# Two model halves on one core: 512-column products and split evictions for the first half's FFN expansions, chunks 5 to 23

## The reference

```
def conv_ffn(x, w_up, conv_w, conv_b, w_down):
    h = causal_dwconv(x @ w_up, conv_w, conv_b)      # w_up 1024 x 6144, conv over 3 positions
    u, g = jnp.split(h, 2, axis=-1)
    return (u * jax.nn.gelu(g)) @ w_down             # w_down 3072 x 1024
...
h = h + conv_ffn(rms_norm(h, ffn_norm_g[l]), ...)    # l = 0, 1
```

## Time and profile before

| what | value |
|---|---|
| three runs | 1871.14, 1871.27, 1871.76 us, median 1871.27 |
| span of the profiled execution, first to last instruction | 1869.4 us |
| TensorE, VectorE, ScalarE, GpSimd busy | 98%, 77%, 52%, 11% of the span |
| instructions | 31793, of them 13284 matmuls |
| memory traffic | 334.67 MB, mean 179 GB/s |

### The profile page before, as it was taken

The page is one execution under the profiler, slowest core; times in us unless marked ns, Lnnn a source line. Parts: engine busy times, 40 slices in busy tenths (PEclk is TensorE's granted clock), DMA queues, the critical chain, the costliest instruction groups (busy, mean ns, idle before and its releaser), DMA issues.

```text
span 1869.4 us, 31793 instructions
## 1 busy us (share of the span) xinstructions
PE 1831.9 (98%) x13284; PEld 1725.2 (92%) x13284; DVE 1436.2 (77%) x1707; ACT 972.1 (52%) x1174; POOL 204.1 (11%) x160
## 2 busy tenths in 40 slices
PE   7999999999999999999999999999999999999997
PEld 7889998999999998899999998889888999999887
DVE  7987996598998578758965797759775896678764
ACT  6356665385665355544453555535553445445542
POOL 2001321000432030002200010001000320001000
PEclk9999999999999999999999999999999999999999
DMA  7324555435555545554454454544555445445551
GB/s 290 133 102 158 190 188 186 181 136 181 192 192 181 203 158 192 203 214 150 166 201 161 158 203 181 202 181 176 186 202 203 158 175 192 155 164 206 191 206 65
DMA packets 46789, 334.67 MB, mean 179 GB/s; under 512 B 5184, under 2 KB 5568, under 8 KB 6464
## 3 DMA queue, kind: packets, MB, share of 16 engines
q1 hardware_dynamic: 46512, 332.20, 49.2%
q0 software_dynamic: 144, 0.52, 0.1%
HBM read 331.65 MB, written 1.05 MB: 178 GB/s over the span
## 4 chain that ended last, share of the span: by engine, by line
PE 82%; DVE 10%; ACT 3%; POOL 2%; DMA 1%; issue 1%; SPq 0%; DVEq 0%; ACTq 0%
PE psum L277 24%; PE psum L280 12%; PE psum L261 11%; PE psum L263 11%; PE psum L262 11%; PE psum L301 6%; DVE w_lo L243 3%; PE psum L308 3%; POOL scratch L1746 1%; DMA w_raw<-stream_in 1%; POOL x_resid L391 1%; ACT w_hi L234 1%; DVE scratch L328 1%; POOL scratch L1743 1%; PE psum L597 1%
## 5 line engine op out<-in xcount | busy, mean ns | idle before, releaser
L234 ACT ACTIVATE w_hi<-w_raw 128x2048 fp32r<-128x2048 f32 x313 | 597.1, 1912 | 422.2 <-PE psum L263 158.1
L243 DVE TENSOR_TENSOR w_lo<-w_raw,w_hi 128x2048 fp32r<-128x2048 f32 x313 | 724.2, 2316 | 39.8 <-ACT w_hi L234 39.8
L261 PE MATMUL psum<-x_split,w_hi 128*128 128x256 f32 x1896 | 541.0, 285 | 13.8 <-DVE x_split L423 10.4
L263 PE MATMUL psum<-x_split,w_lo 128*128 128x256 f32 x1896 | 537.0, 283 | 0.0
L262 PE MATMUL psum<-x_split,w_hi 128*128 128x256 f32 x1896 | 537.0, 283 | 0.0
L277 PE MATMUL psum<-x_split,w_hi 128*128 128x512 f32 x1088 | 384.6, 399 | 0.0
L261 PEld LDWEIGHTS psum<-x_split,w_hi 128*128 128x128 f32 x1896 | 364.4, 192 | 15.2 <-issue 14.6
L262 PEld LDWEIGHTS psum<-x_split,w_hi 128*128 128x128 f32 x1896 | 364.4, 192 | 0.5
L263 PEld LDWEIGHTS psum<-x_split,w_lo 128*128 128x128 f32 x1896 | 364.3, 192 | 0.0
L280 PE MATMUL psum<-x_split,w_lo 128*128 128x256 f32 x1088 | 305.6, 281 | 0.0
L277 PE MATMUL psum<-h_split,w_hi 128*128 128x512 f32 x816 | 288.6, 399 | 0.0
(11 more groups left out here) (249 smaller groups left out, 2411.8 us busy)
## 6 DMA issues: line engine op xcount, KB each, us to landing
w_raw<-stream_in SPq DMA_DIRECT2D x313, 1024.0 KB, 4.8
x_resid<-x_in SPq DMA_DIRECT2D x1, 1024.0 KB, 6.9
y_out<-x_resid SPq DMA_DIRECT2D x4, 256.0 KB, 2.5
scratch<-mask_in SPq DMA_DIRECT2D x1, 768.0 KB, 10.9
scratch<-ev_in SPq DMA_DIRECT2D x1, 512.0 KB, 9.5
scratch<-inv_in POOLq DMA_DIRECT2D x1, 512.0 KB, 6.1
params<-par_in SPq DMA_DIRECT2D x1, 247.0 KB, 7.1
matrices<-mat_in SPq DMA_DIRECT2D x1, 192.0 KB, 8.9
```

The lines of the kernel that those rows point to most:

```text
L234: act.activation(w_hi[:, n % RING, :], raw[:, n % RAWS, :], ACT.Copy).then_inc(hi_ready, 1)
L243: dve.tensor_tensor(w_lo[:, n % RING, :], raw[:, n % RAWS, :], w_hi[:, n % RING, :].bitcast(F32), ALU.subtract).then_inc(lo_ready, 1)
L261: pe.matmul(dst, w_hi[:, c.slot, b:b + P], src[:, k0 + k, 0, :], start=opens, stop=False)
L263: done = pe.matmul(dst, w_lo[:, c.slot, b:b + P], src[:, k0 + k, 0, :], start=False, stop=last and k == nk - 1 and m == len(tiles_) - 1)
```

## The change

`up0` and `up1` join the list of wide phases. Their chunks 5 to 23 (19 in each) are then issued wide, take two events each, and go through the three-step eviction. The count by which the three steps are signalled covers the two new phases, and ScalarE's first tap waits for the scaled sum.

```diff
-WIDE = ("upA", "upB")
+WIDE = ("up0", "up1", "upA", "upB")
...
-FIRST = [("ev_in", 13, 13), ("ev_out", 4, 4), ("up0", FF1, FF1), ("down0", 12, 7),
+FIRST = [("ev_in", 13, 13), ("ev_out", 4, 4), ("up0", FF1, 2 * FF1 - NARROW), ("down0", 12, 7),
...
-         ("up1", FF1, FF1), ("down1", 12, 7)]
+         ("up1", FF1, 2 * FF1 - NARROW), ("down1", 12, 7)]
...
         def wide_count(c):
-            return (WIDE.index(c.phase) + 2 * c.layer) * (FF2 - NARROW) + c.n - NARROW + 1
+            first = {"up0": 0, "up1": FF1 - NARROW, "upA": 2 * (FF1 - NARROW),
+                     "upB": 2 * (FF1 - NARROW) + FF2 - NARROW}[c.phase]
+            return first + 2 * c.layer * (FF2 - NARROW) + c.n - NARROW + 1
...
             def taps(c):
                 w, b = conv
-                act.wait_ge(*taken(c.event))
+                act.wait_ge(*scaled(c))
```

## The result

The changed kernel takes 1881.43 us (median of four runs, 1880.24 to 1882.01) against 1871.20 us before (median of four as well); the ratio is 1.0049, with a 95% interval of 1.0037 to 1.0061. It is slower by 0.5%. The profiled execution took 1880.24 us.

The account below looks back on a forecast made before the run. TensorE was taken to bound the kernel, VectorE right behind it and setting the pace of up0 and up1 after the change. Late starts of 3.88 + 5.16 = 9.04 us on 1871.27 gave 1880.3 us, range 1874.5 to 1884.7.

Parts of the forecast that it names:

- The bound: In up0 and up1 TensorE sets the pace without gaps, VectorE close behind, needing 5.35 us against 5.76 a chunk.
- TensorE's gain of 0.11 us a chunk: In up0 and up1, 38 chunks go from 5.76 to 5.65 us, 4.2 us of gain if nothing else holds TensorE.
- VectorE's period: Per wide chunk of up0 and up1: 5.35 - 0.60 + 1.33 = 6.08 us, over TensorE's 5.65, so VectorE sets the pace.
- GpSimd's share: In up0 and up1, GpSimd's two instructions per chunk lengthen VectorE's four taps from 1.66 to 2.63 us, by 0.97.
- the fourth case: Much slower rival: GpSimd falls on the scaling, 0.38 us each round, period 6.46, loss 21.9 us, 1893 us; chance 0.05.
- Where the waits begin: TensorE waits for banks from chunk 11 of up0 and chunk 8 of up1, some 13 and 16 waits of 0.43 us.
- The hand-over: In up0 and up1, from the end of VectorE's addition to TensorE's start on the freed banks: 0.14 us.
- The starts of the contractions: down0 starts at 294.78, 3.88 us late; down1 at 590.92 against 585.76, 5.16 us late.
- The last hidden tile: Ready at 310.95 in down0, read by TensorE at 311.02; just holds, a miss costing some tenths of a us per phase.
- The sum: Whole kernel: 3.88 + 5.16 = 9.04 us slower, span 1878.4 us, time 1880.3 us.

Follow-up runs that it names:

- experiment 1: The changed kernel without VectorE's scaling in up0 and up1, chunks 5 to 23 left unscaled: 1865.99 us, ratio 0.9968 against the kernel before.
- experiment 2: The changed kernel with GpSimd's two instructions per chunk of up0 and up1 made light (16 of 256 columns; a zero fill): 1867.35 us, ratio 0.9978.
- Experiment 3: The kernel before, products narrow, plus one VectorE instruction of the scaling's size behind each take of chunks 5 to 23 of up0 and up1: 1881.79 us, ratio 1.0057.
- experiment 4: The changed kernel with wide products in up0 and up1, but VectorE taking only left halves and no ScalarE copy there: 1866.72 us, ratio 0.9973.
- experiment 6: The changed kernel with GpSimd's two instructions per chunk of up0 and up1 moved to VectorE, behind the taps: 1869.37 us, ratio 0.9986.
- experiment 7: The changed kernel with GpSimd's two instructions moved to VectorE and the wide form only from chunk 9 of up0 and up1: 1869.47 us, ratio 0.9983.
- experiment 5: The changed kernel with the wide form only from chunk 15 of up0 and up1, 9 chunks in each: 1870.79 us, ratio 0.9990.

## Why the prediction was right

**The bound.** That VectorE stood right behind TensorE in `up0` and `up1` was the step that decided, and it was read from the stretches and from the catching up, not from the page. Experiments 1, 2 and 3 show it: less load on VectorE and the loss is gone, the load alone and the loss is there.

**TensorE's gain of 0.11 us a chunk.** Measured 0.106 (experiment 4, `up0`).

**VectorE's period.** 6.08 forecast, 6.08 measured over sixteen rounds: the take 1.33 us, the taps 2.63 to 2.64. Both durations were lent from `upA` and from the narrow rounds, and both held.

**GpSimd's share.** 0.97 us forecast and 0.97 measured (experiment 2). None of the scalings found in the two phases of the changed kernel is longer than 0.693 us, so GpSimd did not fall on them; that is what kept the fourth case away. The experiments show that GpSimd's two instructions lengthen the taps; by what way they do it, none was made to tell.

**Where the waits begin.** Forecast from chunk 11 of `up0` and chunk 8 of `up1`. Chunk 11 of `up0` is the one at 215.67, which would have started at 215.40; chunk 8 of `up1` is seen in the same way at 497.45. That makes 13 and 16 inside the phases, as forecast; the list of waits leaves out the first of each, and adds the starts of `down0` and `down1`. The break ahead of chunk 6 of `up1` was not foreseen: the sum compared the banks only from the first addition on, and not those that VectorE's last narrow take frees. It cost nothing, since VectorE's lateness is what the phase ends with.

**The hand-over.** 0.14 us was taken from the end of an addition to TensorE's start. It is 287.92 + 0.68 = 288.60 to 288.65, 0.05, and then 0.10 for the longer first matmul. This term is nearly three times what was measured, and only together with the slower first matmul, which the forecast did not know, do the two come out even. That part of the agreement is luck.

**The starts of the contractions.** `down0` 294.78 forecast, 294.73 measured; `down1` 590.92 + 3.88 = 594.80 forecast in the changed kernel's time, 594.76 measured. Together 9.04 forecast and 9.00 measured.

**The last hidden tile** was forecast just in time, ready at 310.95 and read at 311.02. In `down0` it was so: it is ready at 310.78, and no start is late. In `down1` it missed by a little, with the 0.15 us shown above; TensorE came to it early there, because it ran at the quicker pace of the last section. Experiment 3 shows what a later tile costs.

**The sum.** The span was forecast at 1878.4 and is 1878.5 us; the profiled execution 1880.3 against 1880.24. The median of four runs is 1.2 us higher, and only a part of that may be what the last section shows.

## What to carry to other kernels

Before an engine is relieved at another's cost, compare both periods inside the stage, and take the second engine's where it is catching up and never waits: there its true need shows (here 5.35 of 5.76 us, under a page that says 77%). A need over the pace costs nothing until the reserve in buffers is used up, and then costs in full, so the same edit can gain on few iterations and lose on many. Count the price of work on GpSimd in what it takes from VectorE too.

## What the runs showed of the hardware that was not expected

**A short fall of the granted clock in some executions.** In the profiles of experiments 1, 2, 3, 6 and 7 TensorE's granted clock reads 0.97 over one stretch, and 1.00 in those of the kernels before and after and of experiments 4 and 5. The row of experiment 1 for 100 to 150 us, and that of the kernel before (matmul busy time, granted clock, DMA share, GB/s):

```profile
100.00:150.00 50.00, 48.78 (x395) 0.97 0.26 94
```
```profile
100.00:150.00 50.00, 48.78 (x408) 1.00 0.28 100
```

In experiment 1 the fall lies between 120 and 128 us; from 124 to 128 the granted clock reads 0.65, so that it was at the lower of its two levels for most of that time. That stretch is in the attention part, ahead of `up0`, where no kernel here differs. The reciprocal ahead of `up0` then comes at 167.31 instead of 165.69 us, 1.6 us later. Times of one kernel lie in two groups with about this distance, such as 1867.99 to 1868.15 and 1869.47 to 1869.95 us in the eleven runs of experiment 7. It may be part of the 1.2 us between the changed kernel's profiled execution and its median, but not all: of its four runs, the one of 1881.87 us has the same mean clock as the profiled one, 0.998. What starts the fall was not tried.

**Another pace of TensorE.** In the profiles of experiments 1 and 4 the wide chunks of `up1`, from chunk 6 on, and of `down1` take 5.55 us, while those of `up0` take 5.65, with the same instructions and the clock at 1.00. ScalarE's roundings in experiment 1, two in `up0` and two in `up1`:

```profile
240.31 1.91 ACT L234 ACTIVATE w_hi<-w_raw 128x2048 fp32r<-128x2048 f32 x1
...
245.97 1.91 ACT L234 ACTIVATE w_hi<-w_raw 128x2048 fp32r<-128x2048 f32 x1
...
560.13 1.91 ACT L234 ACTIVATE w_hi<-w_raw 128x2048 fp32r<-128x2048 f32 x1
...
565.68 1.91 ACT L234 ACTIVATE w_hi<-w_raw 128x2048 fp32r<-128x2048 f32 x1
```

It is why experiments 1 and 4 gained more than 4.2 us in their profiles: from `down0` to `down1` it is 291.13 and 291.08 us there, and 292.76 in experiment 2, while all three have 123.19 us from the reciprocal to `down0`.

The quicker pace is not theirs alone. In `down1` of the changed kernel ten pairs take 3.47 us, and behind the break at 610.87 ten pairs take 3.53:

```profile
602.15 0.40 PE L277 MATMUL psum<-h_split,w_hi 128*128 128x512 f32 x1
...
605.62 0.40 PE L277 MATMUL psum<-h_split,w_hi 128*128 128x512 f32 x1
...
611.33 0.39 PE L277 MATMUL psum<-h_split,w_hi 128*128 128x512 f32 x1
...
614.86 0.40 PE L277 MATMUL psum<-h_split,w_hi 128*128 128x512 f32 x1
```

Several of the changed kernel's waiting chunks have the quicker pace too, where it gains nothing. In experiment 1 it begins at 481.68, where chunk 6 of `up1` starts 0.05 us after VectorE's take of chunk 4 has ended (480.95 + 0.68), with the longer first matmul that follows a break. Between 180 and 700 us, in the profiles that have it, the pace changes only at such a break of TensorE, though not at every one; the profile of the kernel before has no break in its wide chunks of `down0` and `down1` and stays at 0.353 us a pair. What decides which of the two paces follows a break stays open. The ten runs of experiment 4 spread from 1864.41 to 1869.19 us, which may be this.
